# Adding the prompt's attention bias on VectorE in PSUM in place of an identity matmul

## What is computed

```python
logits = jnp.einsum('bnqgrd,bnkgd->bngrqk', qb, kb).astype(jnp.float32) * (HEAD_DIM ** -0.5)
...
logits = logits + rel_bias_for(d, rel_bias)
logits = jnp.where(valid[:, None, None], logits, NEG_INF)
p = sink_probs(logits, sinks)
out = jnp.einsum('bngrqk,bnkgd->bnqgrd', p.astype(vb.dtype), vb)
```

## Time and profile before

| | |
|---|---|
| time, median of 3 runs | 1348.97 us (1347.09 to 1350.80) |
| the profiled execution | 1346.22 us, span of its slowest core 1344.7 us |
| TensorE busy with matmuls | 1246.0 us (93%), 7798 matmuls |
| VectorE busy | 676.5 us (50%) |
| ScalarE busy | 394.9 us (29%) |
| mean granted TensorE clock, by core | 0.974 to 0.978 |

### The profile page before, as it was taken

How to read it: one execution, slowest core, us unless ns; L and a number is a source line. 1 busy time by engine, 2 the same in 40 slices (tenths; PEclk the granted TensorE clock), 3 DMA queues, 4 the chain that set the end, 5 groups by cost and what they waited for, 6 DMA issues and landing times.

```text
span 1344.7 us, 21758 instructions; the slowest of 8 cores (1337.0 to 1344.7 us)
## 1 busy us (share of the span) xinstructions
PE 1246.0 (93%) x7798; PEld 588.6 (44%) x7798; DVE 676.5 (50%) x1439; ACT 394.9 (29%) x699; POOL 126.5 (9%) x210
## 2 busy tenths in 40 slices
PE   3866999998999999999989899999999899989997
PEld 1322444443545345444435443344444344444445
DVE  2535666555168538843353266568834453222235
ACT  3334321163222442223352113442233341101123
POOL 2111101011000000000110000000011000000000
PEclk9987999999999999999989999999999999999999
DMA  8594554348343334433483253344454267343413
GB/s 190 124 184 154 107 99 87 60 76 94 48 95 85 60 62 81 87 65 66 66 97 51 56 90 63 60 78 88 77 94 81 43 136 158 55 74 69 74 31 126
DMA packets 69960, 117.35 MB, mean 87 GB/s; under 512 B 26136, under 2 KB 36024, under 8 KB 69824
## 3 DMA queue, kind: packets, MB, share of 16 engines
q0 software_dynamic: 43632, 80.79, 38.4%
q1 hardware_dynamic: 26224, 35.18, 8.4%
HBM read 183.39 MB, written 15.37 MB: 148 GB/s over the span
## 4 chain that ended last, share of the span: by engine, by line
PE 77%; DVE 9%; issue 5%; ACT 4%; DMA 3%; SPq 1%; DVEq 0%; ACTq 0%; POOLq 0%
PE ps L204 70%; PE psy L204 6%; ACT L208 1%; DVE xT_s L214 1%; DMA wf<-wgu 1%; DVE hB_s L214 1%; ACT rt_s L208 1%; SPq L82 1%; DVE hA_s L211 1%; DMA scr_tab<-hB_s 1%; DVE mix_s L211 1%; DVE hA_s L214 1%; DVE mix_s L214 1%; DVE hB_s L211 1%; DVE aT_s L211 1%
## 5 line engine op out<-in xcount | busy, mean ns | idle before, releaser
L204 PE MATMUL ps<-hA_s,wf 128*128 128x512 bf16 (+1 forms) x1424 | 325.8, 388 | 40.9 <-ACT sg_s L208 21.6
L204 PE MATMUL ps<-hB_s,wf 128*128 128x512 bf16 (+1 forms) x2112 | 335.1, 319 | 7.8 <-ACT sg_s L208 3.3
L204 PE MATMUL ps<-aT_s,wf 128*128 128x512 bf16 (+2 forms) x1628 | 306.1, 343 | 11.5 <-DVE xT_s L214 9.3
L208 ACT ACTIVATE sg_s<-ps 128x512 f32<-128x512 f32 (+3 forms) x285 | 148.9, 535 | 556.5 <-PE ps L204 485.0
L211 DVE TENSOR_TENSOR aT_s<-ps,sg_s 128x512 bf16<-128x512 f32 (+2 forms) x221 | 130.2, 592 | 320.0 <-PE ps L204 226.4
L204 PEld LDWEIGHTS ps<-hB_s,wf 128*128 128x128 bf16 x2112 | 158.9, 98 | 180.5 <-issue 20.0
L204 PEld LDWEIGHTS ps<-hA_s,wf 128*128 128x128 bf16 x1424 | 140.9, 100 | 218.9 <-issue 65.6
L214 DVE SCALAR_TENSOR_TENSOR xT_s<-ps,xT_s 128x512 f32<-128x512 f32 (+2 forms) x208 | 117.9, 578 | 213.9 <-PE ps L204 213.5
L204 PEld LDWEIGHTS ps<-aT_s,wf 128*128 128x128 bf16 x1628 | 136.8, 98 | 170.6 <-issue 34.1
L82 POOL DMA_DIRECT2D wf<-wgu x88 | 47.0, 534 | 681.4 <-PE ps L204 619.1
L208 ACT ACTIVATE hB_s<-xT_s 128x512 bf16<-128x512 f32 (+2 forms) x104 | 47.1, 475 | 79.2 <-DVE xT_s L214 77.8
(11 more groups left out here) (171 smaller groups left out, 791.3 us busy)
## 6 DMA issues: line engine op xcount, KB each, us to landing
wf<-wgu POOLq DMA_DIRECT2D x88, 512.0 KB, 5.9
wf<-wd POOLq DMA_DIRECT2D x59, 352.0 KB, 4.5
xT_s<-xT SPq DMA_DIRECT2D x6, 1024.0 KB, 11.7
yT<-xT_s SPq DMA_DIRECT2D x12, 512.0 KB, 5.7
scr_tab<-hB_s SPq DMA_DIRECT2D x8, 512.0 KB, 3.9
hA_s<-scr_tab SPq DMA_DIRECT2D x16, 256.0 KB, 4.2
hB_s<-scr_tab SPq DMA_DIRECT2D x16, 256.0 KB, 3.9
wm_s<-wout POOLq DMA_DIRECT2D x12, 256.0 KB, 4.0
```

Source lines behind the costliest of these rows:

```text
L204: return self.P.op('pe', lambda e: e.matmul(out, lhsT, rhs, start=start, stop=stop, skip_group_check=skip), waits=waits, signal=signal)
L208: return self.P.op('act', lambda e: e.activation(out=out, in_=in_, func=func, **kw), waits=waits)
```

## The change

In `scores`, the two score matmuls now open and close their banks by themselves, and VectorE adds the bias to the scores in PSUM, in place, before each Exp. So that the table needs no turning at each use, `setup_gen` turns it once: four identity matmuls into bank 7, each copied back over its quarter of `BT`, with a `yield None` between matmul and copy. Nothing else changes.

```diff
         def scores(n_, kb, ty, sl):
...
+            ts_ = []
             for g in range(2):
-                self.mm(self.ps[SB[g]], self.ident[:], self.BT[:, ty, 4 * g:4 * g + 4, :], True, False,
-                        waits=self.psr[SB[g]] + [self.t_ident] + self.t_tables)
+                gs = slice(64 * g, 64 * g + 64)
+                ts_.append(self.mm(self.ps[SB[g]], self.kT[gs, kb * 128:(kb + 1) * 128], self.q[gs, :, q0:q0 + 128], True, True,
+                                   waits=[self.tok_q[(r, ti)] for r in range(4)] + [self.tok_k[ti], self.tok_k[kb // 4]] + self.psr[SB[g]],
+                                   signal=True))
             out = []
             for g in range(2):
-                gs = slice(64 * g, 64 * g + 64)
-                t_s = self.mm(self.ps[SB[g]], self.kT[gs, kb * 128:(kb + 1) * 128], self.q[gs, :, q0:q0 + 128], False, True,
-                              waits=[self.tok_q[(r, ti)] for r in range(4)] + [self.tok_k[ti], self.tok_k[kb // 4]], signal=True)
+                s4 = self.ps[SB[g]].rearrange("p (r q) -> p r q", r=4)
+                t_s = self.tt(s4, s4, self.BT[:, ty, 4 * g:4 * g + 4, :], ALU.add, waits=[ts_[g]] + self.t_tables)
                 t_e = self.act(self.pT[sl + g], self.ps[SB[g]], AF.Exp, waits=[t_s] + pT_rd[sl + g])
...
         yield vcp(self.BT[:].rearrange("p a h q -> p h a q"), stage.rearrange("p (h a) q -> p h a q", a=2), [t_tp]) or 1.3
+        for i in range(4):
+            bt = self.BT[:, i // 2, 4 * (i % 2):4 * (i % 2) + 4, :]
+            t_m = self.mm(self.ps[7], self.ident[:], bt, True, True, waits=[prev[0], self.t_ident] + self.psr[7], signal=True)
+            yield None
+            yield vcp(bt, self.ps[7].rearrange("p (r q) -> p r q", r=4), [t_m]) or 0.7
+            self.psr[7] = [prev[0]]
         tb = [prev[0]]
```

## The result

The changed kernel takes 1377.4 us (median of 6 runs, 1375.2 to 1378.5), the kernel before 1348.1 (median of 6): a ratio of 1.0214, 95% interval 1.0200 to 1.0227. The change costs 29 us. The forecast was 1363, in a range from 1350 to 1371: slower was right, the size was half of it.

What follows compares the result with a forecast made beforehand. TensorE, busy 93% of the span, was taken to bound the kernel. Terms -4.1 + 2.5 + 2.7 + 7.1 + 3.9 + 1.6 = +13.7 us on the profiled 1346.2 gave 1359.9, or 1363 on the median's scale; range 1350 to 1371.

Steps and rivals of the forecast that it cites:

- Setup: Setup up to the FFN boundary: four added matmuls, moved `kp` batch and moved norms lose 7.1, 3.9 and 1.6 us.
- The four waits: Setup: the turning matmuls wait for VectorE, 1.3 idle once and 1.66 three times; 7.1 us with their own time.
- batch of `kp`: Setup: first `kp` matmuls, moved from slot 60 to 63, wait 3.1, not 0.95, plus 1.7 of clock; 3.9 us lost.
- the boundary: FFN boundary: later norms put two more products ahead of what TensorE awaits, beyond its 2.74 wait; 1.6 us lost.
- Half 0: First half of attention: identity matmuls saved, with TensorE bounding the steps without SSM work; 4.1 us gained in total.
- dense TensorE in half 0: Sign in the changed profile: in 467 to 496, steps shorter by 0.43 with TensorE dense.
- Half 1: Second half of attention: 2.7 us lost at its start and 2.5 us over its six pairs.
- The start: Start of half 1: scores wait for adds, table load and Exp; TensorE idle 5.6 us, start 2.7 us later.
- VectorE bounds: Half 1, six pairs: VectorE's cycles of 6.47 plus 10.5 of SSM make 49.3 us, 2.5 longer than now.
- VectorE has room: Rival: VectorE absorbs the adds, attention gains the full 13.3, setup still costs 12.6; 1348.3 us, chance 0.16.
- And the setup is covered too: Rival: the four setup waits and the shift also find slack, so all 13.3 count; 1335.7 us, chance 0.04.
- Dearer: Rival: clock falls in the four setup waits (6.8), or adds cost 0.1 more (3.6); 1366 to 1370 us, chance 0.14.

Runs made afterwards that it cites:

- e7: Changed kernel with the setup turning spread over eight slots without yields, the output bank copied by ScalarE, and the product one step later; ratio to before 0.9954.
- e11: e7 plus a one-column Exp on ScalarE at the start of each half's attention, to load the table early; ratio to before 0.9949.
- e10: Changed kernel without the SSM's pump in the down groups of attention, its work moving to the stage behind; single time 1392.3 us.
- e6: Changed kernel with one turning matmul or copy at the head of each of eight slots behind the cast, no yields; ratio to before 1.0109.
- e9: Changed kernel with the product moved one step later, behind the next two adds, without ScalarE's copy of the output bank; single time 1412.0 us.
- e12: Kernel before, with a one-column Exp on ScalarE at the start of each half's attention; ratio to before 0.9993.

## Why the prediction was half right

Over the eight cores the profiled executions differ by 29.2: 14.5 in the setup, 2.6 in half 0, 8.0 in half 1, 1.4 behind attention, -0.6 between the stages, and 3.4 ahead of the cast. The last is not the change's: nothing has changed there, and in all kernels the cast lies between 123 and 141, core by core. The profiled execution of before had it at 130.0 in the mean, all others at 131.5 to 135.8. It was an early one: its cores took 1340.7 in the mean, and those of the kernel before 1343 to 1344 in the executions that the experiments are compared with. So 25.9 stands against the prediction's sum of 13.7; the 3 us that the time of the slowest core grew by beyond these 25.9 are not placed.

*Setup, 12.6 forecast, 14.5 measured: right.* The four waits (kernel after, core 0, timeline of TensorE, with the batch of `kp` and the boundary):

```profile
136.18 0.38 PE L204 MATMUL psy<-BT_s,ident_s 128*128 128x512 bf16 x1 [1.29 <-DVE BT_s L223]
...
141.56 0.38 PE L204 MATMUL psy<-BT_s,ident_s 128*128 128x512 bf16 x1 [1.54 <-DVE BT_s L223]
...
272.71 0.38 PE L204 MATMUL psy<-mix_s 128*32 128x32 bf16 x32 [3.30 <-DVE mix_s L223]
...
328.78 4.81 PE L204 MATMUL ps<-hB_s,wf 128*128 128x512 bf16 x15 [3.76 <-ACT sg_s L208]
```

1.29 and three times 1.54 (1.3 and 1.66 forecast), `kp` 3.30 with a half clock behind it (3.1 and 1.7), the boundary 1.0 longer than the 2.74 of the earlier trace rows (1.6 forecast; 0.6 longer on six of the eight cores). The clock stayed at 1.00 from 136 to 152, as the prediction took it from the earlier trace rows. What was missed: behind the longer wait at the boundary the half clock cost 1.7 more on six of the eight cores, and TensorE had a few shorter waits for VectorE, 0.3 to 1.1 each. The moved DMAs cost nothing, as forecast: TensorE waits 9.0 for `wgu` and 1.2 for `wd`, before 9.8 and 1.0.

*Half 0, 4.1 gained forecast, 2.6 lost: wrong; here lies 6.7 of the 12.2 that are missing.* The step that failed is "TensorE's part becomes 7.03; VectorE's is 6.67 [...]. TensorE bounds: 8 steps gain 3.4 us". It took the longer of two lists, each as if the other engine were always ready; the four pairs took 8.08 to 8.31 there, from wait to wait, and 8.08 is the length of the loop. Its slack could be read before: in the earlier trace rows the product ends at 479.80, and the next output matmuls start 0.42 later (kernel before, core 0, timeline of TensorE):

```profile
480.22 0.41 PE L204 MATMUL psy<-sg_s,mix_s 128*64 128x512 bf16 x2
```

Of the 0.42 the hand-over takes 0.15 (496.65 to 496.80 above). Two adds of 0.60 ahead of the sink's add have no room there. The prediction followed two rounds, one in VectorE's list and one through Exp and the scores' banks, and not the one through the output's bank; and for its own sentence that "the residuals wait behind it on VectorE" it set no price in half 0. Of the signs that it gave for attention, the dense TensorE in half 0 did not come, and in half 1 it is the output matmuls that wait, for the product, and not the score matmuls. Opening the loop (e7 against the change) is worth 8.0 in half 0 and 10.8 in half 1; half 0 is then 5.4 shorter than before. A smaller part is the second step's wait for Exp, 1.24 at the table load where 0.2 was forecast; e11 takes 1.0 of that wait back.

*Half 1, 5.2 lost forecast, 8.0 measured (2.1 of it half clock): the size near, the reason wrong.* The start was right: 5.64 idle on TensorE (5.6 forecast), the table load at 842.50 only behind the first add, and the first two steps 3.4 longer (11.53 before, 14.90 now) for 2.7 (kernel after, core 0, timeline of VectorE, ScalarE and TensorE):

```profile
841.74 1.28 DVE L211 TENSOR_TENSOR ps<-ps,BT_s 128x512 f32<-128x512 f32 x2
842.50 1.28 ACT L208 ACT_TABLE_LOAD   x1 [2.81 <-DVE ps L211]
...
844.53 1.07 PE L204 MATMUL ps<-mix_s 64*128 64x512 bf16 x2 [5.64 <-ACT sg_s L208]
```

Six pairs took 50.24 for 49.3. But "VectorE bounds", from 6.47 and 1.75 of SSM a pair, is refuted by e10 (pairs of 8.07 without SSM) and by e7 (41.27 with all of it). The sum came near by luck: the loop's 8.07 happens to lie by the 8.2 that the prediction gave a pair of VectorE's list.

*Behind attention, nothing forecast, 1.4 measured:* the wait of 1.93 in the earlier trace rows became 2.10, and the clock fell behind it on seven cores; before it did on four. That makes some 0.8 of the 1.4, and the rest is not placed. (The kernel after, core 0: stretch and granted clock.)

```profile
922.50:924.50 2.00, 2.00 (x6) 0.50 0.00 0
```

*The rivals.* "VectorE has room" gave the full 13.3 to attention, and the changed kernel doesn't show it. What it said of VectorE is true all the same, once nothing on it waits for Ln and Exp (e7). The rule that stood beside it, of the Trainium skill (Perfetto Trace Analysis, Identifying the Most-Contended Engine: optimize the engine of the highest occupancy first), did not hold for the change as the prediction read it: 62 matmuls fewer on an engine at 93%, and 2.1% more time. (That section of the Trainium skill warns against judging TensorE by its matmul share, and takes its floating-point work against the peak and its weight loads instead; the weight loads were busy for 44%, VectorE for 50%, and read like that it speaks against loading VectorE.) The Trainium skill (Perfetto Trace Analysis, Optimization Strategy) says next to look for the gaps on that engine and for what releases them, and that is how the loop was found here, in the table of waits. "And the setup is covered too" fell with the four waits. "Dearer" had the adds at 0.1 more, and they took 0.689; or the clock falling in the four setup waits, and it stayed at 1.00. The 65 ns between SBUF and PSUM, estimated from the Trainium skill (Perfetto Trace Analysis, Optimizing Scalar/DVE Operations), do not show: two adds in PSUM take 1.29 back to back, two products in SBUF 1.28.

## What to carry to other kernels

When work moves from a full engine to one that looks half idle, the longer of the two lists is only a lower bound: follow every bank and buffer that passes between the two round until it comes back, add up that round, and look in the trace of before how much slack each hand-over has. An operation that waits for a third engine in the middle of an in-order list is the place to look first: put the next step's work ahead of it, and free what it holds by other means, both at once, since neither alone gained anything here. A producer and its consumer that are emitted in the same slot meet as a wait; one slot apart, and without the yields that moved other work (5.8), the same four matmuls and copies cost 1.7 to 3.2 (e11, e6, e7) instead of 14.3.

## What the runs showed of the hardware

- VectorE adds in place in PSUM at the price of an operation from PSUM to SBUF: 128x512 in 0.689 (0.691 in the earlier trace rows), two of them 0.60 apart.
- TensorE's waits of 1.29 and three of 1.54 between 136 and 152 in the kernel after, and of 1.30 every 8.07 in e10, left the granted clock at 1.00. Waits of 2.42 in e9 went either way: behind one the clock was 0.63 in the mean of 3 us, behind another 1.00. So did waits of 1.93: the clock fell behind them on four cores of the kernel before, on seven of e11 and on none of e7.
- A table load of 1.28 on ScalarE, brought forward, shortened TensorE's wait from 5.64 to 4.37 in half 1 of e11, where ScalarE waited for the adds ahead of Exp; in e12, where it did not, the wait stayed (2.41 before, 2.50).
